# Attention in pairs of heads with four score banks and the scaling of the probabilities on GpSimd, in a fp32 transformer kernel

## The reference, cut to what matters

```python
def softmax_attend(q, k, v, scale):
    s = jnp.einsum('bqhd,bkhd->bhqk', q, k, preferred_element_type=jnp.float32) * scale
    p = jax.nn.softmax(s, axis=-1).astype(v.dtype)
    return jnp.einsum('bhqk,bkhd->bqhd', p, v)
```

## Time and profile before

| | us |
|---|---|
| median of 3 runs | 2407.88 |
| lowest and highest run | 2405.9 and 2411.49 |
| span of the profiled execution | 2408.9 |
| PE busy with matmuls in the span | 2139.8 (89%) |
| DVE busy | 1199.2 (50%) |
| ACT busy | 858.7 (36%) |
| POOL busy | 198.9 (8%) |

### The profile page before, as it was taken

One profiled execution on the slowest core, in us unless ns is written; L12 is line 12 of the kernel. 1 busy time (PEld: TensorE's weight loads), 2 busy tenths in 40 slices (PEclk: granted clock), 3 DMA queues, 4 the chain that ended last, 5 costly groups with the idle time before them and its releaser, 6 DMA issues.

```text
span 2408.9 us, 31965 instructions
## 1 busy us (share of the span) xinstructions
PE 2139.8 (89%) x12424; PEld 1713.1 (71%) x12424; DVE 1199.2 (50%) x2038; ACT 858.7 (36%) x1366; POOL 198.9 (8%) x192
## 2 busy tenths in 40 slices
PE   4999899799989999998898979899978579966998
PEld 2777557347757777775784736789967579966997
DVE  5323344454454333334434464565666675666665
ACT  3422342253232222222433434343344643433343
POOL 0000000000110003003000000200330310031001
PEclk7999899899999999998998989999989899987999
DMA  8426104012534454645381322855532345523563
GB/s 282 141 66 212 53 12 141 28 53 88 175 105 158 168 182 141 201 147 174 117 259 53 124 66 82 271 180 180 187 122 71 122 132 167 182 89 121 165 186 105
DMA packets 280888, 331.53 MB, mean 138 GB/s; under 512 B 13319, under 2 KB 229821, under 8 KB 280765
## 3 DMA queue, kind: packets, MB, share of 16 engines
q1 hardware_dynamic: 268736, 323.05, 41.1%
q10 hardware_dynamic: 12028, 6.79, 1.1%
HBM read 328.77 MB, written 1.05 MB: 137 GB/s over the span
## 4 chain that ended last, share of the span: by engine, by line
PE 69%; DVE 10%; issue 10%; ACT 4%; DMA 3%; POOL 2%; ACTq 0%; POOLq 0%; DVEq 0%
PE ps L465 17%; PE ps L467 17%; PE ps L466 17%; PE ps L1153 3%; PE ps L342 3%; PE ps L1131 2%; DVE SL L429 2%; PE ps L1140 1%; ACT SH L423 1%; DVE SM L1224 1%; DMA RAW<-in_ffn_w 1%; PE ps L352 1%; PE ps L1300 1%; POOL S L649 1%; POOL SQ L647 1%
## 5 line engine op out<-in xcount | busy, mean ns | idle before, releaser
L429 DVE TENSOR_TENSOR SL<-RAW,SH 128x1024 fp32r<-128x1024 f32 (+3 forms) x464 | 530.7, 1147 | 898.4 <-ACT SH L423 897.2
L423 ACT ACTIVATE SH<-RAW 128x1024 fp32r<-128x1024 f32 (+3 forms) x464 | 448.9, 973 | 1074.6 <-PE ps L467 926.8
L465 PE MATMUL ps<-AH,SH 128*128 128x256 f32 (+1 forms) x2048 | 675.2, 330 | 79.1 <-DVE AL L869 29.4
L466 PE MATMUL ps<-AL,SH 128*128 128x256 f32 (+1 forms) x2048 | 666.5, 325 | 0.0
L467 PE MATMUL ps<-AH,SL 128*128 128x256 f32 (+1 forms) x2048 | 665.5, 325 | 0.0
L465 PEld LDWEIGHTS ps<-AH,SH 128*128 128x128 f32 x2048 | 399.9, 195 | 143.7 <-issue 49.4
L467 PEld LDWEIGHTS ps<-AH,SL 128*128 128x128 f32 x2048 | 399.5, 195 | 29.3
L466 PEld LDWEIGHTS ps<-AL,SH 128*128 128x128 f32 x2048 | 400.1, 195 | 27.5
L465 PE MATMUL ps<-HH,SH 128*128 128x256 f32 (+1 forms) x992 | 309.3, 312 | 7.6 <-DVE HL L739 3.8
L467 PE MATMUL ps<-HH,SL 128*128 128x256 f32 (+1 forms) x992 | 308.1, 311 | 0.0
L466 PE MATMUL ps<-HL,SH 128*128 128x256 f32 (+1 forms) x992 | 307.4, 310 | 0.0
(11 more groups left out here) (235 smaller groups left out, 2206.4 us busy)
## 6 DMA issues: line engine op xcount, KB each, us to landing
SIDE<-in_w_mod SPq DMA_DIRECT2D x45, 2048.0 KB, 8.1
RAW<-in_ffn_w SPq DMA_DIRECT2D x64, 1024.0 KB, 5.4
RAW<-in_w_in SPq DMA_DIRECT2D x44, 1024.0 KB, 5.8
RAW<-in_w_ffn_gate SPq DMA_DIRECT2D x22, 1024.0 KB, 10.2
RAW<-in_w_ffn_up SPq DMA_DIRECT2D x22, 1024.0 KB, 5.9
RAW<-in_w_ffn_down SPq DMA_DIRECT2D x16, 1024.0 KB, 5.6
RAW<-in_w_branch SPq DMA_DIRECT2D x24, 512.0 KB, 3.7
RAW<-in_w_out SPq DMA_DIRECT2D x8, 1024.0 KB, 5.4
```

The source lines that it names most:

```text
L423: e.activation(SH[:, m, 0:kt, :], RAW[p][:, 0:kt, o:o + P], ACT.Copy).then_inc(K.up("weight_high"), 1)
L429: e.tensor_tensor(SL[:, m, 0:kt, :], RAW[p][:, 0:kt, o:o + P], SH[:, m, 0:kt, :].bitcast(F32), ALU.subtract).then_inc(K.up("weight_low"), 1)
L465: e.matmul(ps, SH[:, m, k, :], xh, start=k == 0, stop=False)
L466: e.matmul(ps, SH[:, m, k, :], xl, start=False, stop=False)
```

## The change

Steps now run in the order stream, pair of heads, query tile, head of the pair. So two steps that follow each other belong to the even and the odd head. The scores use four banks (6, 7, 2, 3) by n modulo 4 and are issued four steps ahead, the turns use two banks (5, 1), and the outputs of a pair one whole bank each (4 and 0, by turns). The values of both heads are issued together, matmul by matmul in turn, for output partitions 0 to 63 and 64 to 127. The row sums and their reciprocals have four columns each. DVE computes the reciprocal two steps behind the maximum, and the scaling of PR is POOL's. Order of PE: scores 0 to 3; then for each even n turn(n), turn(n+1), the values of the pair before if n is a multiple of 4 from 4 on, scores(n+4), scores(n+5). Order of ACT: exponentials of n and n+1, then copies of the turns n-2 and n-1.

```diff
+        SCORES = (6, 7, 2, 3)
+        TURNED = (5, 1)
+        OUT = (4, 0)
-            self.steps = [(s, h, qt) for s in range(streams) for h in range(HEADS) for qt in range(2)]
+            self.steps = [(s, 2 * hp + j, qt) for s in range(streams) for hp in range(HEADS // 2) for qt in range(2)
+                          for j in range(2)]
+            self.pairs = len(self.steps) // 4
...
-            for b in (4, 5, 6, 7):
+            for b in range(8):
                 reader, count = K.bank[b]
                 e.wait_ge(sem[reader], K.value(reader, count))
...
             def scores(n):
                 s, h, qt = self.steps[n]
+                if n >= 4:
+                    e.wait_ge(sem["exp_done"], K.at("exp_done", n - 3))
+                q, k = self.qk(s, h, qt)
+                e.matmul(self.scores_of(n), q, k, start=True, stop=True).then_inc(K.up("scores_done"), 1)
+
+            def turn(n):
+                c0, c1 = self.keys(self.steps[n][0])
+                e.wait_ge(sem["probs_ready"], K.at("probs_ready", n + 1))
                 if n >= 2:
-                    e.wait_ge(sem["exp_done"], K.at("exp_done", n - 1))
...
+                    e.wait_ge(sem["turned_copied"], K.at("turned_copied", n - 1))
+                for j in range((c1 - c0) // P):
+                    ins = e.transpose(PS[self.TURNED[n % 2]][:, j * P:(j + 1) * P], PR[:, n % 2, j * P:(j + 1) * P],
+                                      IDENT)
+                ins.then_inc(K.up("probs_turned"), 1)
+
+            def values(pair):
+                s, h, _ = self.steps[4 * pair]
                 c0, c1 = self.keys(s)
...
+                e.wait_ge(sem["turned_copied"], K.at("turned_copied", 4 * pair + 4))
+                if pair >= 2:
                     e.wait_ge(sem["branch_low"], K.at("branch_low", pair - 1))
...
+                o = PS[self.OUT[pair % 2]]
                 tiles = (c1 - c0) // P
                 for j in range(tiles):
...
+                    for i in range(2):
+                        ins = e.matmul(o[64 * i:64 * i + 64, 0:256], V[:, c0 // P + j, 64 * (h + i):64 * (h + i) + 64],
+                                       PTS[:, i, j, :], start=j == 0, stop=j == tiles - 1)
                 ins.then_inc(K.up("values_done"), 1)
 
...
+            for n in range(4):
+                scores(n)
+            for n in range(0, n_steps, 2):
                 turn(n)
...
+                turn(n + 1)
+                if n >= 4 and n % 4 == 0:
+                    values(n // 4 - 1)
+                if n + 4 < n_steps:
+                    scores(n + 4)
+                    scores(n + 5)
+            values(self.pairs - 1)
+            for b in self.OUT:
+                K.bank[b] = ("branch_low", K.s("branch_low") + self.pairs)
...
-            for n in range(n_steps + 1):
+            for n in range(0, n_steps + 2, 2):
                 if n < n_steps:
                     exp(n)
-                if n >= 1:
+                    exp(n + 1)
+                if n >= 2:
+                    turned(n - 2)
                     turned(n - 1)
...
+            def invert(n):
                 e.wait_ge(sem["exp_done"], K.at("exp_done", n + 1))
...
+                e.reciprocal(SM[:, 9 + n % 4:10 + n % 4], SM[:, 4 + n % 4:5 + n % 4]).then_inc(K.up("sums_inverted"), 1)
...
-            for n in range(n_steps + 1):
+            for n in range(n_steps + 2):
                 if n < n_steps:
                     maximum(n)
-                if n >= 1:
-                    normalise(n - 1)
...
+                if n >= 2:
+                    invert(n - 2)
...
+        def pool(self, e, K):
+            for n, (s, h, qt) in enumerate(self.steps):
+                c0, c1 = self.keys(s)
+                pr = PR[:, n % 2, 0:c1 - c0]
+                e.wait_ge(sem["sums_inverted"], K.at("sums_inverted", n + 1))
+                e.tensor_scalar(pr, pr, SM[:, 9 + n % 4:10 + n % 4], None, ALU.mult).then_inc(K.up("probs_ready"), 1)
```

More of the change, by code:

```diff
@@ L173 @@
            "vectors_turned"],
-    "pool": ["pool_done", "gated_done", "pooled_last"],
+    "pool": ["pool_done", "gated_done", "pooled_last", "probs_ready"],
 }
@@ L1126, in scores @@
                 s, h, qt = self.steps[n]
-                if n >= 2:
-                    e.wait_ge(sem["exp_done"], K.at("exp_done", n - 1))
-                q, k = self.qk(s, h, qt)
-                c0, c1 = self.keys(s)
[L1131 to L1141, removed]
@@ L1155, in values @@
                 ins.then_inc(K.up("values_done"), 1)
[L1157 to L1161, removed]
-                turn(n)
[L1163 to L1167, removed]
@@ L1170, in outputs @@
+            for b in self.TURNED:
+                K.bank[b] = ("turned_copied", K.s("turned_copied") + n_steps)
+            for b in self.SCORES:
+                K.bank[b] = ("exp_done", K.s("exp_done") + n_steps)
         def outputs(self, pair):
             s = self.steps[4 * pair][0]
-            return pair % 4, slice(s * SEQ, (s + 1) * SEQ), slice(256 * (pair % 2), 256 * (pair % 2) + 256)
+            return pair % 4, slice(s * SEQ, (s + 1) * SEQ), PS[self.OUT[pair % 2]][:, 0:256]
         def act(self, e, K):
@@ L1177, in exp @@
             def exp(n):
-                s, h, qt = self.steps[n]
-                c0, c1 = self.keys(s)
+                c0, c1 = self.keys(self.steps[n][0])
                 e.wait_ge(sem["max_done"], K.at("max_done", n + 1))
@@ L1223, in maximum @@
                     e.wait_ge(sem["dve_done"], K.own("dve_done"))
[L1224 to L1229, removed]
+                e.tensor_reduce(SM[:, n % 4:n % 4 + 1], ps, AX.X, ALU.max, negate=True).then_inc(K.up("max_done"), 1)
+            def invert(n):
                 e.wait_ge(sem["exp_done"], K.at("exp_done", n + 1))
-                e.reciprocal(SM[:, 4 + n % 2:5 + n % 2], SM[:, 2 + n % 2:3 + n % 2]).then_inc(K.up("dve_done"), 1)
-                e.wait_ge(sem["dve_done"], K.own("dve_done"))
-                pr = PR[:, n % 2, 0:c1 - c0]
-                e.tensor_scalar(pr, pr, SM[:, 4 + n % 2:5 + n % 2], None, ALU.mult).then_inc(K.up("probs_ready"), 1)
+                e.reciprocal(SM[:, 9 + n % 4:10 + n % 4], SM[:, 4 + n % 4:5 + n % 4]).then_inc(K.up("sums_inverted"), 1)
@@ L1244, in dve @@
                 if n < n_steps:
                     maximum(n)
-                if n >= 1:
-                    normalise(n - 1)
-                if n >= 6 and (n - 6) % 4 == 0:
-                    out((n - 6) // 4)
-            for pair in range((n_steps - 6) // 4 + 1, n_steps // 4):
-                out(pair)
+                if n >= 2:
+                    invert(n - 2)
+                if n >= 9 and n % 4 == 1:
+                    out((n - 9) // 4)
+            for pair in range((n_steps - 8) // 4 + 1, self.pairs):
+                out(pair)
```

51 lines of the change are left out of this document (21 added, 30 removed).

## The result

The changed kernel takes 2526.33 us (2519.02 to 2528.55, 4 runs) where the kernel before takes 2408.06 us: 1.0487 times as long, with a 95% interval of 1.0469 to 1.0504, so 113 to 121 us slower. The direction was forecast, the size was not: 2440 us, with a range that ended at 2474. The profiled execution has a span of 2526.7 us.

What follows compares the result with a forecast made beforehand. PE's own work was taken to bound the kernel before. Loop +20.7, ends +4 and clock +8 us sum to +32.7 us on a median of 2407.88: about 2440 us, with 2406 to 2474 expected to hold it 8 times in 10.

Steps and rivals of the forecast that it cites:

- The closed loop: Four attention sections: turns wait for GpSimd's scaling and an inversion queued behind the newest scores' maximum; +20.7 us.
- The scaling's price: GpSimd's scaling of PR in the loop: taken as 1.04 us for 128x512, between 0.62 and 1.29 us.
- The clock: The two neighbourhood sections stay longer at 1.2 GHz after their start: +8 us, bounds 0 and +20 us.
- The ends: Behind each of four sections the next unit's first product waits 1.0 us for DVE to empty bank 0: +4 us.
- Packing on PE: Values of two heads run together in column halves: 1.87 us for both instead of 2 x 1.87 us.
- The row halves: Neighbourhood scores of two heads in different row halves: 0 to 0.85 us saved per pair of steps, counted as nothing.
- DVE and GpSimd: DVE's two-tile operations, which might disturb POOL, were said to be absent in the loop; counted as nothing.
- Slow GpSimd and the low clock: Rival: scaling takes 1.29 us and the neighbourhood sections' clock term is at its upper bound; 2465 us, chance 0.17.
- Fast scaling: Rival: GpSimd's scaling takes 0.62 us or under, shortening the loop; 2408 to 2421 us, chance 0.21.
- The loop stays open: Rival: PE sets the attention sections' period, scores(n+4) ending before exp(n+2) does; 2360 us, chance 0.06.
- The halves don't run together: Rival: the two heads' values don't overlap on PE and take 3.74 us per pair; 2477 us, chance 0.06.

Runs made afterwards that it cites:

- version 7: The changed kernel with GpSimd's scaling written as a two-operand product, the inverted sum repeated along the row: 2457.1 us, 1.0208 of before.
- Version 4: The changed kernel with four unused matmuls of 256 columns added per two steps to keep PE busy: 2486.33 us, 1.0315 of before.
- version 12: The changed kernel with both the two-operand scaling on GpSimd and the four added matmuls that keep PE busy: 2435.27 us, 1.0106 of before.
- versions 8 and 9: 8: output banks swapped in the changed kernel, 2525.53 us. 9: swapped, each bank's last reader counted, on the changed kernel with DVE scaling ahead of maxima, 2345.53 us.
- versions 2 and 3: The changed kernel with the scaling back on DVE: 2 keeps the changed order, 2442.8 us; 3 puts scalings ahead of maxima, 2349.02 us.

## Why the prediction was right in sign and wrong in size

The prediction failed at two terms of its sum: GpSimd's price of a scaling and the clock. The order's loop, the ends and the packing came as forecast. The four corners, as time over the kernel before (its 2408 us times the ratio less one; the 95% intervals are 113 to 121, 72 to 80, 41 to 59 and 21 to 30 us, by rows):

| scaling of 128x512 on GpSimd | PE idles in the loop | PE kept busy |
|---|---|---|
| 1.56 us, as changed | +117.3 us | +75.9 us |
| 1.04 us, as I took it | +50.1 us | +25.5 us |

- **The closed loop: right,** in place and in length. The reciprocal stands behind a maximum, PE waits for GpSimd in each half, and with my price and full clock the wide periods are 11.04 us against 11.10 (latent) and 12.42 against 12.57 (neighbourhood). Only the 256-key period was too short: 6.6 us forecast, 6.90 in version 7 (560.52 to 567.42, at a mean clock of 0.88). With these three periods the sum of the loop is 6 x 1.58 + 6 x 1.12 + 8 x 0.69 = 21.7 us where I had 20.7. That the corner with my price and a busy PE is +25.5 where loop and ends were forecast at 24.7 is closer than it deserves: it holds the 1 us or so by which the added matmuls lengthen a narrow pair, and the neighbourhood sections are not at full clock in it.
- **The scaling's price: the first step that failed.** "... and 1.29 the high end; I take 1.04, the row with the same shape and one tile". It is 1.563 us, and 0.922 for 128x256 where I had 0.62. The nearest rows were of two-operand instructions, and the bounds were drawn as if a form that reads less could not take longer. By the same working the true price adds 0.85 us to each of 12 wide neighbourhood halves (0.52 for the first turn, and 1.56 in place of 1.23 for the second), 1.04 to each of 12 latent ones and up to 0.60 to each of 16 narrow ones: 10 + 12.5 + 9.6 = 32 us, estimated. The latent part of it can be measured: versions 4 and 12, both at full clock there, differ by 9.86 + 7.57 = 17.4 us in the latent sections, where this working gives 17.3 (it may be a few us more, since the added matmuls lengthen the narrow pairs of version 12). By the same estimate the rest of the 67 us between the rows of the left column is clock.
- **The clock: the second step that failed,** and the larger. I added 8 us, at most 20 for both neighbourhood sections at 1.2 GHz throughout, and nothing for the latent ones, because the clock was low only at their start before. I had written that PE idles 2.6 us in each half and then priced only a later rise. Idle time in every half lets the clock fall again and again, in the latent sections too. Keeping PE busy gives back 41 us at the true price and 25 at mine, and not all is given back, since the neighbourhood sections stay at 0.67 to 0.89 even then. Of the 117 us some 25 are thus loop and ends as forecast and some 32 the longer scaling, by my estimate; 60 remain. Version 4 shows 31 of them to be clock in the latent sections. Another 21 or so are what the neighbourhood sections lose over the 12 us of loop and 15 us of longer scaling that the working gives them; that these are clock is inferred from their 0.61 and not shown, and they alone exceed my bound of 20. The last few us are not assigned; most of them lie outside the sections.
- **The ends: right,** 1.03 us in four sections, at the place forecast. That bank 0 was the last pair's was only half of the reason: versions 8 and 9 show that the count had to be mended as well.
- **Packing on PE: right,** 1.87 us for two heads where it was 2 x 1.87. The Trainium skill (TensorEngine Tiling (Array Packing), Theoretical Speedup) promises up to twofold for dimensions of 64 or less, and these rows agree. The row halves, priced at nothing, show too: the neighbourhood scores of both heads take 1.13 us together, two of the same size one after the other took 2.1.
- **DVE and GpSimd: a slip without effect.** I wrote that DVE's two-tile operations are absent in the loop. They are there: the bias add (302.00) and the subtraction for YL. But GpSimd's scalings take 3.10 us for two in every wide half of the first section, so no price of theirs shows.
- **The rivals.** *Slow GpSimd and the low clock* was the case that came, with chance 0.17, at 2465 us: right in both causes and short in both sizes. *Fast scaling* is refuted. It rested on X*X reading its tile twice. The Trainium skill (GPSIMD Engine Reference, Engine selection) states that one-input elementwise work is roughly line-rate there, and these runs do not bear it out for this instruction: the one-input form took 1.563 us, 3.2 times the 0.486 us of DVE in versions 2 and 3, and half as long again as the two-operand form. *The loop stays open* was the right figure for another kernel: 2360 us forecast, 2349 measured once DVE's order opens the loop. *The halves don't run together* is refuted by the 1.87 us for both heads.

## What to carry to other kernels

Extra banks give no lookahead if an in-order queue puts the release of the old step behind work on the newest: write each engine's order down and look for the circle, then put what releases others first. When a loop makes PE wait in every round, price the clock in every round, not once at its start. Take the duration of a moved instruction from a row of that same instruction form on that engine; where there is none, the bound is open above, and a probe of both forms is worth more than any neighbouring row.

## What the runs showed that I had not expected

- On GpSimd a multiplication of an fp32 tile by a per-partition column takes 1.563 us (128x512) and 0.922 us (128x256) as TENSOR_SCALAR, but 1.039 and 0.612 us as TENSOR_TENSOR with the column repeated.
- Adding matmuls whose results are never used made the kernel 40 us faster. 31 us of it are the latent sections, whose granted clock rose from 0.65 and 0.71 to 1.00.
- Value passes of two column halves overlap for half their length even when one head's eight are issued wholly ahead of the other's.
